# A HGRN2 head scan whose read-out is computed with tokens on the partitions

## The chip, the cores and the metric

One core of one Trainium2 chip. The metric is the device time of one execution in microseconds. The kernel before was run three times; a fourth execution was profiled.

## What is computed

A two-layer backbone over 512 latent and 256 context tokens of width 1024, all float32. Layer 0 mixes tokens with a bidirectional HGRN2, layer 1 with a Mamba-2; a SwiGLU FFN ends each. The change touches layer 0's mixer alone, 8 heads with keys and values of 128 and chunks of 64 tokens. Each direction computes

```python
cum = jnp.cumsum(lf, axis=2)
ref = cum[:, :, CHUNK // 2 - 1:CHUNK // 2]
qr = qc * jnp.exp(cum - ref)
kr = kc * jnp.exp(ref - cum)
att = jnp.where(causal, jnp.einsum('bclhd,bcshd->bchls', qr, kr), 0.0)
o_intra = jnp.einsum('bchls,bcshv->bclhv', att, vc)
ds = jnp.einsum('bcshd,bcshv->bchdv', kc * jnp.exp(last - cum), vc)
# s_in: the states, scanned over chunks with decay exp(last)
o_inter = jnp.einsum('bclhd,bchdv->bclhv', qc * jnp.exp(cum), s_in)
o = (o_intra + o_inter)
```

and the read-out is `rmsnorm(o_forward + o_backward, gn_w) * silu(g)`, the norm over a head's 128 values, and then a product with `w_out`.

## The kernel before

Activations lie feature-major: 128 features on the partitions, 768 tokens (T) along the free dimension. A weight panel is 128 output features of a weight, loaded by SP (`load_panel`, line 248), split into a rounded high part by ScalarE (`split_hi`, 254) and a low part by VectorE (`split_lo`, 258), and multiplied by `product` (261 to 284): for each of eight k steps three products of high and low parts in two halves of 384 tokens, so six matmuls on line 275. Splits run two panels ahead.

A head needs five panels, j = 0 to 4: q, gate, two forget gates, v. `hg_all` (711) is a software pipeline: while the panels of head h + 1 (called `hn_` there) are multiplied, TensorE does the scan of head h in between, after the k steps that the tables `STEP_AT` and `OUT_AT` (549, 550) name as (j, k). Heads run in pairs in a loop of three turns (`Fori`, 715); the first head has no scan beside it, and the scan of the last has no panels beside it.

The scan's steps on TensorE (`hg_tensor_scan`, 474 to 525): 1 transposes v, 2 and 3 transpose the decayed keys kd of both directions (490), 4 makes the attention blocks (503: 32-column strips of the array), 5 to 7 the state increments of chunks (515, 64 rows of the array each, even and odd chunks in different halves). VectorE masks and adds the attention of both directions into `attS` (670, 674) and runs the states into `sin` (`states`, 636 to 647).

The read-out (`hg_tensor_out`, 527 to 545) gives per chunk of 64 tokens one product with `vtm` as the stationary and `attS` as the moving operand, and one per direction with a state `sin` stationary and 64 columns of `qe` moving:

```python
pe.matmul(to, m["vtm"][o:o + CH, c // 2, :], m["attS"][o:o + CH, c // 2, :], start=True, stop=False)
for d in inter:
    ins = pe.matmul(to, sin[d][:, c, :], chunks(qe[d][:, :])[:, c, :], start=False, stop=(d == inter[-1]))
```

The profile has two records per float32 matmul. The first chunk of a direction has no state, so two of the twelve chunks have one direction. Then ScalarE copies the output to `osb` (631) and squares it into `osq` (632); TensorE sums over partitions with `ones` (step 9, 520); VectorE makes the mean (`mean_dve`, 391), GpSimd the -1/2 power (`rsqrt_pool`, 396), TensorE spreads it over partitions with the identity (`spread_pe`, step 10, 386), and VectorE multiplies twice (705, 708) into `og`. Step 9 stands after (4, 4) and step 10 after (4, 7).

VectorE in panel j = 4, in this order (680 to 709): the split, lf and th (684, 688), the two scans `cum` (694, waiting for ScalarE's Ln, 626), four offsets `kr`, `kd` (699) that ScalarE's exponentials (`decays`, 601 to 607) wait for, then the read-out's mean and the two multiplications. Step 1 of the next head waits for them (`og0`).

Of the kernel before, what the change touches and what calls it, by code (L numbers as in the profile page):

```python
# [25 lines left out]
P = 128  # L26
# [14 lines left out]
HEADS = 8  # L41
# [74 lines left out]
def memory(nc):  # L116
# [4 lines left out]
    def run(at, *items):  # L121
# [31 lines left out]
        *[(n, (P, T)) for n in ("qs", "vT", "osb", "osq")],  # L153
        *[(n, (P, NBLK, P)) for n in ("vtm", "kdtm0", "kdtm1")],
        *[(n, (P, NBLK, CH)) for n in ("att0", "att1", "attS")],
# [24 lines left out]
def program(nc, x, c, ctx_x, c_ctx, ada_w, ada_b, norm_w, ffn_w_in, ffn_w_out, final_norm_w, hg_w_in, hg_lb,  # L180
            hg_norm_w, hg_w_out, ssm_w_in, ssm_conv_w, ssm_conv_b, ssm_dt_bias, ssm_a_log, ssm_d, ssm_norm_w,
            ssm_w_out, out):
    with ExitStack() as ctx:
# [13 lines left out]
            sig lf cum dif ex kd qk vtm kdtm step cp att sf sb osq og0 og osp_hi osp_lo  # L197
# [183 lines left out]

        def spread_pe(pe, K, nb, to):
# [7 lines left out]
        def mean_dve(dve, nb, n):  # L390
            dve.tensor_scalar(m["stat"][:, 0:nb], S[:, 0, 0:nb], 1.0 / n, EPS, ALU.mult, ALU.add)\
               .then_inc(s["stat"], 1)
# [19 lines left out]
        def norm_dve(dve, xt, N, K, segs, l, i):  # L412
            sums_dve(dve, N, segs)
            dve.wait_ge(s["rbc"], K + 1)
# [42 lines left out]
        def by_parity(buf):  # L457
            return buf[:, :].rearrange("p (b q l) -> p q b l", q=2, l=CH)
# [15 lines left out]
        def hg_tensor_scan(pe, hp, h, step):  # L474
# [42 lines left out]
            elif step == 9:  # L517
                pe.wait_ge(s["osq"], h + 1)
                for b in range(NBLK):
                    ins = pe.matmul(S[:, 0, b:b + 1], block(m["osq"][:, :], b), ones[:, :],  # L520
                                    start=True, stop=True)
            else:
                spread_pe(pe, h + 1, NBLK, pair)
                return
            ins.then_inc(s["step"], 1)

        def hg_tensor_out(pe, h, n):

            c = OUT_ORDER[n]
# [17 lines left out]
        OUT_ORDER = sorted(range(NCH), key=lambda c: max(ORDER[0].index(c), ORDER[1].index(c)))  # L547
        OUT_EARLY = sum(max(ORDER[0].index(c), ORDER[1].index(c)) <= 8 for c in range(NCH))
        STEP_AT = {(0, 5): 1, (1, 0): 2, (1, 3): 3, (1, 6): 4, (2, 1): 5, (2, 3): 6, (2, 5): 7, (4, 4): 9, (4, 7): 10}
        OUT_AT = {(3 + (k - 1) // KT if k else 2, (k - 1) % KT): k for k in range(NCH)}  # L550
# [22 lines left out]
        def hg_scalar(act, hg, hn_, hp, h, pn_par, ps_par):  # L573
# [35 lines left out]
            for j in range(5):  # L609
# [40 lines left out]
        def hg_vector(dve, hg, hn_, hp, h, pn_par, ps_par):  # L650
            for j in range(5):
# [14 lines left out]
                if j == 1 and h is not None:  # L666
                    step_done(dve, h, 4)
                    dve.memset(m["carry"][:, :], 0.0)
                    for d in (0, 1):
# [4 lines left out]
                    dve.tensor_tensor(m["attS"][:, :, :], att[0][:, :, :], att[1][:, :, :], ALU.add)\  # L674
                        .then_inc(s["att"], 1)
# [14 lines left out]
                if j == 4 and hg is not None:  # L690
# [473 lines left out]
        def ss_vector(dve, ss, g, q, prev):  # L1164
            for j in range(len(PANELS)):
# [255 lines left out]
        def l1_vector(dve):  # L1421
# [22 lines left out]
            dve.wait_ge(s["rbc"], K2 + 3 + GROUPS)  # L1444
# [70 lines left out]
        def _(pool):  # L1515
# [30 lines left out]
            pool.wait_ge(s["og"], HEADS)  # L1546
# [6 lines left out]
        def _(act):  # L1553
# [13 lines left out]
            act.wait_ge(s["og"], HEADS)  # L1567
# [11 lines left out]
        def _(dve):  # L1579
# [130 lines left out]
```

## Time and profile before

| | |
|---|---|
| median of three runs | 2448.22 us (2442.34 to 2449.22) |
| the profiled execution | 2440.77 us, span 2439.0 us |
| granted TensorE clock over it | 0.945 |
| TensorE busy | 2244.6 us, 92% |
| VectorE, ScalarE busy | 1066.7 us, 843.4 us |
| line 275, three products | 718.1, 668.7 and 668.5 us |
| line 542, states | 64.7 us in 352 records |
| line 540, attention | 44.5 us in 192 records |

Times in rows are from the span's start. A record's length contains its way through the array, so records overlap and starts tell the pace; a busy TensorE is not one at its peak. "Idle before, releaser" says how long an engine had nothing to do and what ended it. The granted clock is a share of full speed: 1.00 is 2.4 GHz, 0.50 is 1.2 GHz.

### The profile page before, as it was taken

The page shows a single profiled execution, that of the slowest core. Times are in us where ns is not written, and L with a number is a line of the kernel's source. Part 1 is how long each engine was busy: PE and PEld are TensorE (multiplying, and loading weights), DVE is VectorE, ACT ScalarE, POOL GpSimd, SP SyncE. Part 2 cuts the span into 40 slices and gives each one's busy share as a digit, 9 for nine tenths or more (in the row PEclk, how much of TensorE's full clock was granted, in tenths as well). Part 3 has the DMA queues.
Part 4 walks back from the last instruction along what each step waited for, and adds up shares of the span by engine and source line. Part 5 has one row for each costly group of instructions (what it writes and reads, how often), then busy time and mean ns, then how long its engine had stood idle before and what let it go on. Part 6 is the DMA issues. An engine that isn't in the chain of part 4 may idle for free.

```text
span 2439.0 us, 34378 instructions
## 1 busy us (share of the span) xinstructions
PE 2244.6 (92%) x13554; PEld 1967.2 (81%) x13554; DVE 1066.7 (44%) x1484; ACT 843.4 (35%) x1250; POOL 39.3 (2%) x67
## 2 busy tenths in 40 slices
PE   5899999998897999999999599999997698999998
PEld 3888888887796999999999587777774476888886
DVE  5444454455334222222223756766665434333333
ACT  2443343443123332112221343737372223542222
POOL 1000000000000000000000100000000000000000
PEclk8999999999698999999999889999998598999998
DMA  6322222222222332234321121121111132332331
GB/s 261 104 79 79 70 66 66 70 64 67 78 78 93 105 112 86 61 104 129 109 74 50 52 70 44 44 61 43 52 43 43 68 102 68 98 103 87 95 111 62
DMA packets 296560, 198.03 MB, mean 81 GB/s; under 512 B 4900, under 2 KB 288925, under 8 KB 295837
## 3 DMA queue, kind: packets, MB, share of 16 engines
q1 hardware_dynamic: 293965, 180.03, 24.1%
q0 software_dynamic: 2512, 16.80, 1.8%
q8 instruction: 64, 1.05, 0.2%
q14 instruction: 19, 0.16, 0.0%
HBM read 186.32 MB, written 10.49 MB: 81 GB/s over the span
## 4 chain that ended last, share of the span: by engine, by line
PE 64%; issue 24%; DVE 7%; ACT 2%; DMA 1%; POOL 1%; SPq 0%; DVEq 0%; ACTq 0%; POOLq 0%
PE G L275 50%; PE G L308 2%; PE S L542 1%; PE S L1296 1%; PE S L386 1%; PE S L1147 1%; DVE hn L420 1%; PE S L540 1%; DVE hlo L428 1%; PE S L515 1%; PE S L1143 1%; PE S L1309 1%; POOL rstd L396 1%; ACT whi L254 1%; PE S L1298 1%
## 5 line engine op out<-in xcount | busy, mean ns | idle before, releaser
L275 PE MATMUL G<-hhi,whi 128*128 128x384 f32 (+1 forms) x2320 | 718.1, 373 | 39.2 <-DVE hlo L428 24.5
L258 DVE TENSOR_TENSOR wlo<-raw,whi 128x1024 fp32r<-128x1024 f32 (+1 forms) x225 | 288.2, 1281 | 934.4 <-ACT whi L254 934.4
L275 PE MATMUL G<-hhi,wlo 128*128 128x384 f32 (+1 forms) x2320 | 668.7, 351 | 0.0
L275 PE MATMUL G<-hlo,whi 128*128 128x384 f32 (+1 forms) x2320 | 668.5, 351 | 0.0
L254 ACT ACTIVATE whi<-raw 128x1024 fp32r<-128x1024 f32 (+1 forms) x225 | 248.9, 1107 | 1025.7 <-PE G L275 507.5
L275 PEld LDWEIGHTS G<-hhi,whi 128*128 128x128 f32 x2320 | 416.2, 192 | 99.3 <-issue 52.7
L275 PEld LDWEIGHTS G<-hhi,wlo 128*128 128x128 f32 x2320 | 429.8, 191 | 20.8
L275 PEld LDWEIGHTS G<-hlo,whi 128*128 128x128 f32 x2320 | 431.3, 191 | 18.0
L275 PE MATMUL G<-mhi,whi 128*128 128x384 f32 (+1 forms) x656 | 209.1, 362 | 13.7 <-DVE mlo L1428 13.7
L275 PE MATMUL G<-mlo,whi 128*128 128x384 f32 (+1 forms) x656 | 208.7, 361 | 0.0
L275 PE MATMUL G<-mhi,wlo 128*128 128x384 f32 (+1 forms) x656 | 208.5, 361 | 0.0
L275 PEld LDWEIGHTS G<-mhi,whi 128*128 128x128 f32 x656 | 121.2, 189 | 26.8 <-issue 11.5
L275 PEld LDWEIGHTS G<-mlo,whi 128*128 128x128 f32 x656 | 121.2, 189 | 12.0
L275 PEld LDWEIGHTS G<-mhi,wlo 128*128 128x128 f32 x656 | 121.1, 188 | 11.9
L1178 DVE SCALAR_TENSOR_TENSOR acc<-xpad,colC,acc 128x770 f32<-128x770 f32 (+1 forms) x96 | 93.7, 976 | 36.4 <-ACT acc L1064 29.1
L1036 ACT ACTIVATE e<-S,shiftT 128x128 f32<-128x128 f32 x256 | 69.5, 382 | 57.6 <-PE S L1298 57.4
L772 ACT ACTIVATE mhi<-mid 128x768 f32 (+3 forms) x44 | 32.5, 739 | 95.8 <-DVE mid L793 95.8
L542 PE MATMUL S<-qe,sin 128*128 128x64 f32 x352 | 64.7, 307 | 0.0
L647 DVE SCALAR_TENSOR_TENSOR sin<-sin,gl,S 128x128 f32<-128x128 f32 x160 | 54.9, 348 | 6.9 <-PE S L515 1.8
L542 PEld LDWEIGHTS S<-qe,sin 128*128 128x128 f32 x352 | 50.9, 206 | 7.0
L347 ACT ACTIVATE sq<-x 128x512 f32 (+3 forms) x32 | 23.5, 738 | 93.3 <-DVE x L821 66.5
L797 DVE TENSOR_TENSOR mlo<-mid,mhi 128x768 f32 (+3 forms) x44 | 36.3, 826 | 44.2 <-ACT mhi L772 44.2
(245 smaller groups left out, 2025.3 us busy)
## 6 DMA issues: line engine op xcount, KB each, us to landing
raw<-in_ffn_w_in_dram SPq DMA_DIRECT2D x88, 512.0 KB, 3.6
adaw<-in_ada_w_dram SPq DMA_DIRECT2D x40, 1024.0 KB, 5.3
raw<-in_ffn_w_out_dram SPq DMA_DIRECT2D x32, 704.0 KB, 4.2
raw<-in_ssm_w_in_dram SPq DMA_DIRECT2D x41, 512.0 KB, 3.6
raw<-in_hg_w_in_dram SPq DMA_DIRECT2D x40, 512.0 KB, 3.7
ada<-in_ada_w_dram SPq DMA_DIRECT2D x4, 2048.0 KB, 13.1
raw<-in_ssm_w_out_dram SPq DMA_DIRECT2D x16, 512.0 KB, 3.4
raw<-in_hg_w_out_dram SPq DMA_DIRECT2D x8, 512.0 KB, 3.5
```

What stands on the lines that cost most here:

```text
L254: act.activation(whi[pn.slot][:, 0:kt, :], raw[pn.slot][:, 0:kt, :], ACT.Copy).then_inc(s["hi"], 1)
L258: dve.tensor_tensor(wlo[pn.slot][:, 0:kt, :], raw[pn.slot][:, 0:kt, :], f32(whi[pn.slot][:, 0:kt, :]), ALU.subtract).then_inc(s["lo"], 1)
L275: ins = pe.matmul(G[:, tl.slot, g0:g0 + n], w[pn.slot][:, k, :], r[:, k_base + k, t0:t0 + n], start=(first and k == 0 and i == 0), stop=(l ...
L308: ins = pe.matmul(to[o:o + 2, :], m["csil"][:, k, :], w[:, k, :], start=(k < STRIPS), stop=(k >= KT - STRIPS))
L386: ins = pe.matmul(block(to, b), m["rstd"][:, b:b + 1].to_broadcast([P, P]), ident[:, :], start=True, stop=True)
L396: pool.tensor_tensor(m["rstd"][:, 0:nb], m["stat"][:, 0:nb], m["mhalf"][:, 0:nb], ALU.pow)\
L542: ins = pe.matmul(to, sin[d][:, c, :], chunks(qe[d][:, :])[:, c, :], start=False, stop=(d == inter[-1]))
L647: dve.scalar_tensor_tensor(to, sin[d][:, cc, :], gl[d][:, cc:cc + 1], new, ALU.mult, ALU.add).then_inc(own, 1)
L772: act.activation(m["mhi"][:, bass.ds(i, 1), 0:nt].rearrange("p a t -> p (a t)"), m["mid0"][:, 0:nt], ACT.Copy).then_inc(s["mhi"], 1)
L797: dve.tensor_tensor(m["mlo"][:, bass.ds(i, 1), 0:nt].rearrange("p a t -> p (a t)"), m["mid0"][:, 0:nt], f32(m["mhi"][:, bass.ds(i, 1), 0:n ...
L1036: ins = act.activation(block(m[f"e{d}{r}"][:, :], b), block(S[:, d, :], b), ACT.Exp, bias=m["shiftT"][:, b, bass.ds(q * HPG + (d * NH + hh ...
L1178: dve.scalar_tensor_tensor(m["acc"][:, 0:n], xpad[ci % 2][:, k:k + n], m["colC"][:, bass.ds(conv_tile(kind, i, g) + k * CONV_TILES, 1)], m ...
```

## The change

The read-out is written for a block of 128 tokens, two chunks, with tokens on the partitions. `attS` becomes 128 x 128 per block, with each chunk's 64 x 64 on the diagonal and zeros elsewhere (set once ahead of head 0), and is the stationary operand; `vtm` is moving. For the states, 64 columns of `qe` are stationary and the state moves with 128 columns; the even chunk uses array columns 0 to 63, the odd one 64 to 127. Mean squares are then sums along the free dimension: ScalarE squares straight from PSUM into the buffer of `vT`, VectorE reduces, and scales with `rstd` broadcast along the free dimension. Six transposes bring the result back to feature-major, and one operation applies weight and gate. Steps 9 (sums) and 10 (spread) and the `osb` copy go. `OUT_AT` puts the six blocks into panels 2 and 3.

```diff
+        *[(n, (P, T)) for n in ("qs", "vT", "osb")], ("osum", (P, 8)),
+        *[(n, (P, NBLK, CH)) for n in ("att0", "att1")], ("attS", (P, NBLK, P)),
...
+        osq = m["vT"]
...
-            elif step == 9:
-                pe.wait_ge(s["osq"], h + 1)
+            else:
+                pe.wait_ge(s["osn"], h + 1)
                 for b in range(NBLK):
-                    ins = pe.matmul(S[:, 0, b:b + 1], block(m["osq"][:, :], b), ones[:, :],
-                                    start=True, stop=True)
-            else:
-                spread_pe(pe, h + 1, NBLK, pair)
-                return
+                    ins = pe.transpose(block(pair, b), block(m["osb"][:, :], b), ident[:, :])
...
-            elif n == OUT_EARLY:
+            elif n == NBLK - LBLK:
...
-            o = CH * (c % 2)
-            to = S[:, 2 + c % 2, (c // 2) * CH:(c // 2 + 1) * CH]
-            inter = [d for d in (0, 1) if c != ORDER[d][0]]
-            pe.matmul(to, m["vtm"][o:o + CH, c // 2, :], m["attS"][o:o + CH, c // 2, :], start=True, stop=False)
-            for d in inter:
-                ins = pe.matmul(to, sin[d][:, c, :], chunks(qe[d][:, :])[:, c, :],
-                                start=False, stop=(d == inter[-1]))
-            if n == NCH - 1:
+            to = block(PAIR[1], b)
+            pe.matmul(to, m["attS"][:, b, :], m["vtm"][:, b, :], start=True, stop=False)
+            for d in (0, 1):
+                for c in (2 * b, 2 * b + 1):
+                    if c != ORDER[d][0]:
+                        o = CH * (c % 2)
+                        ins = pe.matmul(to[o:o + CH, :], chunks(qe[d][:, :])[:, c, :], sin[d][:, c, :],
+                                        start=False, stop=(d == 1 or c == ORDER[1][0]))
+            if n == NBLK - 1:
...
-        STEP_AT = {(0, 5): 1, (1, 0): 2, (1, 3): 3, (1, 6): 4, (2, 1): 5, (2, 3): 6, (2, 5): 7, (4, 4): 9, (4, 7): 10}
-        OUT_AT = {(3 + (k - 1) // KT if k else 2, (k - 1) % KT): k for k in range(NCH)}
+        OUT_ORDER = list(range(LBLK, NBLK)) + list(range(LBLK))
+        STEP_AT = {(0, 5): 1, (1, 0): 2, (1, 3): 3, (1, 6): 4, (2, 1): 5, (2, 3): 6, (2, 5): 7, (4, 7): 9}
+        OUT_AT = {(2, 7): 0, (3, 1): 1, (3, 3): 2, (3, 4): 3, (3, 5): 4, (3, 6): 5}
...
-                    act.activation(by_parity(m["osb"]), o4, ACT.Copy)
-                    act.activation(by_parity(m["osq"]), o4, ACT.Square).then_inc(s["osq"], 1)
+                    act.activation(osq[:, :], PAIR[1][:, 0:T], ACT.Square).then_inc(s["osq"], 1)
...
-                    dve.tensor_tensor(m["attS"][:, :, :], att[0][:, :, :], att[1][:, :, :], ALU.add)\
-                        .then_inc(s["att"], 1)
+                    for o in (0, CH):
+                        ins = dve.tensor_tensor(m["attS"][o:o + CH, :, o:o + CH], att[0][o:o + CH, :, :],
+                                                att[1][o:o + CH, :, :], ALU.add)
+                    ins.then_inc(s["att"], 1)
...
+                if j == 4 and h is not None:
+                    dve.wait_ge(s["osq"], h + 1)
+                    dve.tensor_reduce(m["osum"][:, 0:NBLK], by_block(osq[:, :]), axis=mybir.AxisListType.X,
+                                      op=ALU.add).then_inc(s["osr"], 1)
+                    dve.wait_ge(s["osr"], h + 1)
+                    mean_dve(dve, NBLK, P, m["osum"][:, 0:NBLK])
+                if j == 4 and hg is not None:
+                    offsets(hn_, 0)
+                if j == 4 and h is not None:
+                    dve.wait_ge(s["rstd"], h + 2)
+                    r = m["rstd"][:, 0:NBLK].rearrange("p (b a) -> p b a", a=1)
+                    dve.tensor_tensor(by_block(m["osb"][:, :]), by_block(PAIR[1][:, 0:T]),
+                                      r.to_broadcast([P, NBLK, P]), ALU.mult).then_inc(s["osn"], 1)
+                if j == 4 and hg is not None:
+                    offsets(hn_, 1)
                 if j == 4 and h is not None:
                     step_done(dve, h, 9)
-                    mean_dve(dve, NBLK, P)
-                    dve.wait_ge(s["rbc"], h + 2)
-                    dve.scalar_tensor_tensor(m["osb"][:, :], m["osb"][:, :], m["colA"][:, COL_GN:COL_GN + 1],
-                                             PAIR[1][:, 0:T], ALU.mult, ALU.mult).then_inc(s["og0"], 1)
-                    dve.wait_ge(s["og0"], h + 2)
-                    dve.tensor_tensor(m["og"][:, bass.ds(h, 1), :].rearrange("p a t -> p (a t)"),
-                                      m["osb"][:, :], gs[ps_par][:, :], ALU.mult).then_inc(s["og"], 1)
+                    dve.scalar_tensor_tensor(m["og"][:, bass.ds(h, 1), :].rearrange("p a t -> p (a t)"),
+                                             PAIR[0][:, 0:T], m["colA"][:, COL_GN:COL_GN + 1], gs[ps_par][:, :],
+                                             ALU.mult, ALU.mult).then_inc(s["og0"], 1)
...
+            dve.memset(m["attS"][:, :, :], 0.0).then_inc(s["og0"], 1)
```

`offsets(head, d)` holds the two subtractions of line 699 for one direction. The waits on `rbc` elsewhere count eight fewer spreads, and what waited for `og` now waits for `og0`.

TensorE in the fourth panel (j = 3) of a head, before; each row names the moving, then the stationary operand, and the size of the result:

```order
L275 MATMUL G<-hhi,wlo_70 128x384 x2
L540 MATMUL S<-attS,vtm 128x64
L542 MATMUL S<-qe_97,sin_119 128x64
L542 MATMUL S<-qe_98,sin_120 128x64
L275 MATMUL G<-hhi,whi_69 128x384 x2
```

and with the change:

```order
L275 MATMUL G<-hhi,wlo_70 128x384 x2
L542 MATMUL S<-vtm,attS 128x128
L547 MATMUL S<-sin_119,qe_97 64x128 x2
L547 MATMUL S<-sin_120,qe_98 64x128 x2
L275 MATMUL G<-hhi,whi_69 128x384 x2
```

One insertion now holds a block of two chunks; before, each chunk had its own, and three chunks stood in the fifth panel.

VectorE from the second scan to the product into `og`, in the panel j = 4, before:

```order
L694 SCALAR_TENSOR_TENSOR cum_106<-segm,lf_104 128x768
L699 TENSOR_TENSOR kr_93<-cum_105 128x768
L699 TENSOR_TENSOR kd_99<-cum_105 128x768
L699 TENSOR_TENSOR kr_94<-cum_106 128x768
L699 TENSOR_TENSOR kd_100<-cum_106 128x768
L571 REGISTER_ALU
L391 TENSOR_SCALAR stat<-S 128x6
L704 REGISTER_ALU
L705 SCALAR_TENSOR_TENSOR osb<-osb,colA,S 128x768
L708 ISA
L708 TENSOR_TENSOR og<-osb,gs_107 128x768
```

and with the change:

```order
L704 SCALAR_TENSOR_TENSOR cum_106<-segm,lf_104 128x768
L708 TENSOR_REDUCE osum<-vT 128x6
L395 TENSOR_SCALAR stat<-osum 128x6
L656 TENSOR_TENSOR kr_93<-cum_105 128x768
L656 TENSOR_TENSOR kd_99<-cum_105 128x768
L715 REGISTER_ALU
L717 TENSOR_TENSOR osb<-S,rstd 128x768
L656 TENSOR_TENSOR kr_94<-cum_106 128x768
L656 TENSOR_TENSOR kd_100<-cum_106 128x768
L575 REGISTER_ALU
L723 ISA
L723 SCALAR_TENSOR_TENSOR og<-S,colA,gs_107 128x768
```

The reduce and the mean now stand ahead of the offsets of direction 0, the scaling between the two directions, and the product into `og` behind the transposes that wait for the scaling. The offsets are on line 656 now, in `offsets`.

## Rows read from the trace of the kernel before

**Rows 1.** The page: busy time by engine, and the chain by engine.
```profile
PE 2244.6 (92%) x13554; PEld 1967.2 (81%) x13554; DVE 1066.7 (44%) x1484; ACT 843.4 (35%) x1250; POOL 39.3 (2%) x67
...
PE 64%; issue 24%; DVE 7%; ACT 2%; DMA 1%; POOL 1%; SPq 0%; DVEq 0%; ACTq 0%; POOLq 0%
```

**Rows 2.** Windows of single heads (us, PE, PEld, DVE, ACT, POOL busy, PEclk, DMA share, GB/s).
```profile
190.02:261.97 71.95, 68.72 (x564) 62.05 (x563) 37.29 (x57) 25.90 (x36) 1.32 (x1) 0.98 0.23 71
261.97:329.71 67.74, 66.90 (x564) 60.44 (x563) 28.87 (x49) 25.91 (x36) 1.32 (x1) 1.00 0.22 69
```

**Rows 3.** PE timeline (start, length, what, count): a step with a chunk, plain steps.
```profile
302.00 0.51 PE L275 MATMUL G<-hlo,whi 128*128 128x384 f32 x2
...
302.79 0.43 PE L540 MATMUL S<-attS,vtm 64*128 64x64 f32 x2
303.15 0.66 PE L542 MATMUL S<-qe,sin 128*128 128x64 f32 x4
...
304.06 0.51 PE L275 MATMUL G<-hlo,whi 128*128 128x384 f32 x2
...
318.22 0.51 PE L275 MATMUL G<-hlo,whi 128*128 128x384 f32 x2
...
319.26 0.51 PE L275 MATMUL G<-hlo,whi 128*128 128x384 f32 x2
```

**Rows 4.** PE timeline of the fifth panel of that head.
```profile
308.18 0.60 PE L275 MATMUL G<-hhi,whi 128*128 128x384 f32 x2
...
321.99 1.60 PE L386 MATMUL S<-ident,rstd 128*128 128x128 f32 x12 [0.84 <-POOL rstd L396]
323.35 0.59 PE L275 MATMUL G<-hhi,whi 128*128 128x384 f32 x2
```

**Rows 5.** PE timeline, other insertions of the same head.
```profile
338.51 0.82 PE L490 MATMUL S<-ident,kd 128*128 128x128 f32 x6
339.08 0.59 PE L275 MATMUL G<-hhi,whi 128*128 128x384 f32 x2
...
342.41 1.46 PE L503 MATMUL S<-qr,kr 128*32 128x64 f32 x96
...
350.98 1.16 PE L515 MATMUL S<-vtm,kdtm 64*128 64x128 f32 x16
...
354.36 0.94 PE L515 MATMUL S<-vtm,kdtm 64*128 64x128 f32 x12
```

**Rows 6.** VectorE timeline beside that fifth panel.
```profile
310.59 1.02 DVE L684 TENSOR_SCALAR lf<-th 128x768 f32<-128x768 f32 x2
...
313.60 3.41 DVE L694 TENSOR_TENSOR_SCAN cum<-segm,lf 128x768 f32<-128x768 f32 x2 [1.06 <-ACT lf L626]
316.93 0.93 DVE L699 TENSOR_TENSOR kr<-cum 128x768 f32<-128x768 f32 x1
317.78 0.95 DVE L699 TENSOR_TENSOR kd<-cum 128x768 f32<-128x768 f32 x1
...
323.64 1.01 DVE L705 SCALAR_TENSOR_TENSOR osb<-osb,colA,S 128x768 f32<-128x768 f32 x1 [3.10 <-PE S L386]
```

**Rows 7.** ScalarE timeline there.
```profile
314.56 0.81 ACT L631 ACTIVATE osb<-S 128x768 f32<-128x768 f32 x1
```

**Rows 8.** PE windows around a loop branch (us, PE busy, PEclk, DMA share, GB/s).
```profile
391.30:395.05 3.75, 0.04 (x1) 1.00 0.00 0
395.26:398.67 3.41, 3.41 (x12) 0.50 0.56 159
```

**Rows 9.** Timelines of the last head, PE and then VectorE; a window.
```profile
620.14 0.66 PE L540 MATMUL S<-attS,vtm 64*128 64x64 f32 x2 [1.28 <-issue]
...
640.85 2.72 PE L520 MATMUL S<-ones,osq 128*128 128x1 f32 x12 [1.60 <-ACT osq L632]
...
649.24 0.96 DVE L708 TENSOR_TENSOR og<-osb,gs 128x768 f32<-128x768 f32 x1
...
617.15:652.00 34.85, 26.41 (x104) 22.89 (x104) 7.58 (x20) 3.28 (x5) 1.92 (x2) 0.50 0.02 5
```

More of the change, by code:

```diff
@@ L152, in memory @@
         *[(f"{n}{d}", (P, T)) for n in ("kr", "qr", "qe", "kd", "th", "lf", "cum", "gs") for d in (0, 1)],
-        *[(n, (P, T)) for n in ("qs", "vT", "osb", "osq")],
+        *[(n, (P, T)) for n in ("qs", "vT", "osb")], ("osum", (P, 8)),
         *[(n, (P, NBLK, P)) for n in ("vtm", "kdtm0", "kdtm1")],
-        *[(n, (P, NBLK, CH)) for n in ("att0", "att1", "attS")],
+        *[(n, (P, NBLK, CH)) for n in ("att0", "att1")], ("attS", (P, NBLK, P)),
         *[(f"sin{d}", (P, NCH, P)) for d in (0, 1)], *[(f"gl{d}", (P, NCH)) for d in (0, 1)],
@@ L196, in program @@
             x sq sqd ssum stat rstd rbc hn hhi hlo
-            sig lf cum dif ex kd qk vtm kdtm step cp att sf sb osq og0 og osp_hi osp_lo
+            sig lf cum dif ex kd qk vtm kdtm step cp att sf sb osq osr osn og0 osp_hi osp_lo
             mhi mlo
@@ L380, in norm_pe, with spreads @@
             spread_pe(pe, K, nb, PAIR[1])
+        def spreads(K):
+            return K + 1 - (HEADS if K else 0)
         def spread_pe(pe, K, nb, to):
@@ L388, in spread_pe, with mean_dve @@
             ins.then_inc(s["rbc"], 1)
-        def mean_dve(dve, nb, n):
-            dve.tensor_scalar(m["stat"][:, 0:nb], S[:, 0, 0:nb], 1.0 / n, EPS, ALU.mult, ALU.add)\
+        def mean_dve(dve, nb, n, total=None):
+            dve.tensor_scalar(m["stat"][:, 0:nb], S[:, 0, 0:nb] if total is None else total, 1.0 / n, EPS, ALU.mult, ALU.add)\
                .then_inc(s["stat"], 1)
@@ L413, in norm_dve @@
             sums_dve(dve, N, segs)
-            dve.wait_ge(s["rbc"], K + 1)
+            dve.wait_ge(s["rbc"], spreads(K))
             def scaled(j):
@@ L455, in chunks, with by_block @@
             return ap.rearrange("p (c l) -> p c l", l=CH)
-        def by_parity(buf):
-            return buf[:, :].rearrange("p (b q l) -> p q b l", q=2, l=CH)
+        def by_block(ap):
+            return ap.rearrange("p (b n) -> p b n", n=P)
+        osq = m["vT"]
         def at_token(ap, t):
@@ L516, in hg_tensor_scan @@
                                     m["vtm"][o:o + CH, cc // 2, :], start=True, stop=True)
[L517 to L518 removed]
+            else:
+                pe.wait_ge(s["osn"], h + 1)
                 for b in range(NBLK):
[L520 to L524 removed]
+                    ins = pe.transpose(block(pair, b), block(m["osb"][:, :], b), ident[:, :])
             ins.then_inc(s["step"], 1)
         def hg_tensor_out(pe, h, n):
[L529 removed]
+            b = OUT_ORDER[n]
             if n == 0:
@@ L533, in hg_tensor_out @@
                 pe.wait_ge(s["att"], h + 1)
-            elif n == OUT_EARLY:
+            elif n == NBLK - LBLK:
                 for own in ("sf", "sb"):
                     pe.wait_ge(s[own], 11 * h + 11)
-            o = CH * (c % 2)
-            to = S[:, 2 + c % 2, (c // 2) * CH:(c // 2 + 1) * CH]
-            inter = [d for d in (0, 1) if c != ORDER[d][0]]
-            pe.matmul(to, m["vtm"][o:o + CH, c // 2, :], m["attS"][o:o + CH, c // 2, :], start=True, stop=False)
-            for d in inter:
-                ins = pe.matmul(to, sin[d][:, c, :], chunks(qe[d][:, :])[:, c, :],
-                                start=False, stop=(d == inter[-1]))
-            if n == NCH - 1:
+            to = block(PAIR[1], b)
[7 more added lines that the diff above has]
+            if n == NBLK - 1:
                 ins.then_inc(s["step"], 1)
-        OUT_ORDER = sorted(range(NCH), key=lambda c: max(ORDER[0].index(c), ORDER[1].index(c)))
-        OUT_EARLY = sum(max(ORDER[0].index(c), ORDER[1].index(c)) <= 8 for c in range(NCH))
-        STEP_AT = {(0, 5): 1, (1, 0): 2, (1, 3): 3, (1, 6): 4, (2, 1): 5, (2, 3): 6, (2, 5): 7, (4, 4): 9, (4, 7): 10}
-        OUT_AT = {(3 + (k - 1) // KT if k else 2, (k - 1) % KT): k for k in range(NCH)}
+        OUT_ORDER = list(range(LBLK, NBLK)) + list(range(LBLK))
+        STEP_AT = {(0, 5): 1, (1, 0): 2, (1, 3): 3, (1, 6): 4, (2, 1): 5, (2, 3): 6, (2, 5): 7, (4, 7): 9}
+        OUT_AT = {(2, 7): 0, (3, 1): 1, (3, 3): 2, (3, 4): 3, (3, 5): 4, (3, 6): 5}
         def hg_tensor(pe, hg, hn_, hp, h, pn_par, ps_par):
@@ L650, in hg_vector, with offsets @@
         def hg_vector(dve, hg, hn_, hp, h, pn_par, ps_par):
+            def offsets(head, d):
+                dve.wait_ge(s["cum"], 2 * head + d + 1)
+                for to, t in ((kr, REF[d]), (kd, LAST[d])):
+                    dve.tensor_tensor(chunks(to[d][:, :]), chunks(cum[d][:, :]),
+                                      at_token(cum[d][:, :], t), ALU.subtract).then_inc(s["dif"], 1)
             for j in range(5):
@@ L1220, in ss_vector @@
                     mean_dve(dve, LBLK, GW)
-                    dve.wait_ge(s["rbc"], q + (K2 + 2))
+                    dve.wait_ge(s["rbc"], q + spreads(K2 + 1))
                     for i_ in range(GT):
@@ L1443, in l1_vector @@
             sums_dve(dve, 4, LAT)
-            dve.wait_ge(s["rbc"], K2 + 3 + GROUPS)
+            dve.wait_ge(s["rbc"], spreads(K2 + 2 + GROUPS))
             for j in range(KT):
@@ L1545, in _ @@
                 rsqrt_pool(pool, h + 1, NBLK)
-            pool.wait_ge(s["og"], HEADS)
+            pool.wait_ge(s["og0"], HEADS + 1)
             pool.wait_ge(s["parked0"], 16)
@@ L1566, in _ @@
             hg_all(act, lambda *a: hg_scalar(act, *a))
-            act.wait_ge(s["og"], HEADS)
+            act.wait_ge(s["og0"], HEADS + 1)
             for j in range(HEADS):
@@ L1624, in _ @@
             for d in (0, 1):
-                ins = dve.memset(att[d][:, :, :], 0.0)
-            ins.then_inc(s["og0"], 1)
+                dve.memset(att[d][:, :, :], 0.0)
+            dve.memset(m["attS"][:, :, :], 0.0).then_inc(s["og0"], 1)
             dve.wait_ge(s["og0"], 1)
```

6 lines of the change are left out of this document (removed).

## The prediction

> **What bounds the kernel now.** I read the page first. TensorE is busy for 92% of the span and the chain that ended last runs mostly through it [rows 1], so work taken off TensorE counts where nothing is put in its place. Then I read the windows of single heads. From one head's value transposes to the next takes 67.74 us, and PE is busy for 66.90 of it; where the loop branches back the same stretch takes 71.95 us [rows 2]. TensorE bounds all of the head loop. The PE timeline prices what the change replaces.
>
> I measure an insertion between panel products from one hlo row to the next. A plain step of six L275 takes 319.26 - 318.22 = 1.04 us; the step that holds one chunk's read-out takes 304.06 - 302.00 = 2.06 us [rows 3]. A chunk costs 1.02 us, and one of a single direction 0.22 less, since its two L542 records are missing and the four of the row last 0.66 us at 0.11 us from start to start. Of the twelve chunks of a head, nine stand ahead of the fifth panel (j = 4) and three in it: 7 x 1.02 + 2 x 0.80 = 8.7 us and 3.06 us. The fifth panel runs from 308.18 to 323.35 [rows 4], 15.17 us: eight plain steps 8.32, three chunks 3.06, and the 3.79 left are the sums (L520) and the spread (L386), 0.84 of it idle until GpSimd's rstd.
>
> **The read-out.** A block of two chunks is now one full-array product (two records, 0.11 each, 0.22) and two pairs of 64-column products. The price of a pair that runs side by side is in the state products, which use two halves of the array's rows in the same manner: sixteen records last 1.16 us, twelve 0.94 [rows 5], so a pair (four records) costs 0.22. Four records one after another, with 128 streamed columns each, would be 0.43. That products in different columns overlap too is seen at L503: 96 records in four column strips last 1.46 us [rows 5], and one after another, with 48 columns on the mean at 0.11 for 128, they would be 3.9. Two pairs make 0.44. Changing the array's shape, in and out, I take from the chunk: of its 1.02 the six records are 0.66 at 0.11, which leaves 0.36, say 0.4. A block: 0.22 + 0.44 + 0.4 = 1.05 us; bounds 0.9 (smaller weight loads) and 1.5 (no overlap). Six blocks are 6.3 us, all ahead of the fifth panel, against 8.7: **2.4 us per head** there.
>
> **The fifth panel and its new wait.** Now nothing stands in it but eight plain steps: PE is through at 308.18 + 8.32 = 316.5 in this head's times, and stops at the six transposes for osn. Who makes osn? VectorE's scans start at 313.60 and keep it until 316.9, when the first offset starts [rows 6]; they wait for ScalarE's logarithms, which hang on the end of the fourth panel and don't move against it. The Square needs no more waiting for the read-out and fits where the osb copy was, 314.56 to 315.4 [rows 7]. Then on VectorE: the reduce of 128x768; stat 0.2 with the waits between; the two offsets of direction 0, 0.85 from start to start [rows 6], to about 319.9; the scaling from PSUM 1.0 (as L705 [rows 6]), to 321.0. GpSimd's 1.32 [rows 2] lies beside the offsets. The reduce isn't in the trace. Its bounds are 0.5, half of the two single-source passes of L684 in 1.02, and 1.7, half of the two scans [rows 6]; I take 0.95, as the passes over two tensors with the same 768 columns. The Trainium skill (VectorE: DVE Perf Modes, the perf-mode tier table) speaks against this operation: `tensor_reduce` has only its 1x mode, while a one-source fp32 pass can have 2x. By it the low end is out; at the price of a one-source pass the wait would be 0.4 shorter. No row here shows a reduce.
>
> So PE stands from 316.5 to 321.0, **4.5 us where it stood 0.84**. The transposes take what L490 takes, 0.57 to the next L275 [rows 5], so the next head begins at 321.6 and not 323.35: 1.8 us saved. Together 4.2 us per head.
>
> **The clock.** After a PE gap of 3.75 us at the loop's branch the granted clock was 0.50 for 3.41 us, in which 12 matmuls ran [rows 8], 0.28 us each against 0.17 in a plain step. Gaps of 0.84 were followed by none (clock 1.00 over a whole head [rows 2]). A gap of 4.5 us in each head will be followed by such a stretch: half of 3.41 is 1.7 us. Net 2.5 us per head. The branch back comes on top in two heads, where one slow stretch is paid already.
>
> **Who is behind the new wait.** ScalarE's decays of direction 0 start 1.1 us later (the reduce and stat stand ahead of the offsets), as its inputs do; VectorE's offsets of direction 1 end at 322.6 and og at 323.6, against 325.6 now. The next vT transposes come five steps after the wait, some 327: covered. Panel splits are two panels ahead. POOL's rstd and SP's loads have nothing new in front of them. If the five steps went, vT's transposes would wait for og. The attS sum becomes two half-height passes (about 0.5 us more) five steps or more ahead of its use; the memset of attS, no longer than a pass of 768 columns, lies ahead of head 0, under its panels. Both cost nothing there, and 0.5 once in the last head.
>
> **The last head** has no panels, so its chain is paid in full and at half clock: read-out from 620.14 to 639.2 (the sums start at 640.85 after 1.60 idle), 19.1 us; from there the square, the sums, the spread and two products until 650.2, 11.0 us; the clock is 0.50 [rows 9]. New: a block at half clock 0.43 + 0.86 + 0.4 = 1.7, six 10.2: 8.9 saved. Then Square 0.8, reduce 0.95, stat 0.3, rstd 1.4, scaling 1.0, six transposes at half clock 1.5, og 1.0: 7.0, against 11.0: 4.0 saved. VectorE enters this head about 2.0 earlier against the fourth panel, less 0.5 for attS: 1.5. Together 14.4 us.
>
> **Sum.** 2.4 (first head's read-out) + 6 x 2.5 = 15 + 14.4 = 31.8 us. The profiled execution took 2440.8 and would take 2409.0; the median of the three runs is 2448.2, 7.4 above it, and I keep that distance: **2416.5 us**.
>
> **The rivals.**
> *The clock takes a second slow stretch in each head* (0.13). The wait, the transposes and in two heads the branch stand in a row; 1.7 x 6 = 10 more: 2427. For it: in the last head gaps of 1 to 2 us keep the clock at 0.50 [rows 9]. Against: 3.75 us of gap cost one stretch only. The Trainium skill (TensorE: Matmul & The Clock Gate, PE-mode transpose) says that transposes don't count as busy for the clock in the way matmuls do; by it the wait and the transposes are one gap of 5.1 us, and 2427 would be the likelier time. A head of the kernel before, with 18 transposes among its panels, ran at 1.00 [rows 2], which neither bears it out nor speaks against it.
> *The clock holds* (0.08), as after 0.84: 10 less, 2406.
> *Column pairs run one after another* (0.10): each block 0.43 dearer, 2.6 a head over seven heads is 18, and at half clock 5 in the last: about 2440. Against it stands L503.
> *Each change of column half empties the array* (0.04), the case on the other side. Then each of four products costs as a lone one does: L540's 0.36 to the next start [rows 3] and 0.05 for its 128 columns, 0.41. A block is 0.22 + 1.65 + 0.2 = 2.05, dearer than its chunks; a head's six 12.3 against 6.3, 6.0 more in each of seven heads is 42, and some 10 more in the last: 2416.5 + 52 = 2468. It decides from 1.65 us a block, where the gain of 32 is spent. Against it: L503 changes strips with each record and shows nothing of this. The Trainium skill (TensorEngine Tiling (Array Packing), Key Properties) says that a change of mode drains the engine and a change of tile does not; by it this case doesn't occur and only my 0.4 per block does.
> Something I don't see has 0.03.
>
> **How the numbers follow.** The forecast as costed has 0.62. About 7 us (0.3%) is what a measurement of this kernel can tell from no change. The first three cases are faster; of the column case (8 us) half; so faster 0.88, same 0.07, slower 0.05. The range reaches from 2403 (clock holds, a cheap reduce and blocks of 0.95) to 2436 (second stretch, reduce of 1.7, half of the column loss); above lie most of the column case and the slower one.
>
> **What would show it.** Right: blocks near 1.05 us; at the osb transposes an idle of about 4.5 us released by the scaling; a 0.50 clock after it in each head; a period near 65 us; last read-out near 10 us. Wrong: periods over 67, two slow stretches a head, or four block products with starts 0.2 or more apart.

## The result, and the profile after

| | before | changed |
|---|---|---|
| median | 2445.56 us (four runs, 2442.34 to 2449.22) | 2408.3 us (four runs, 2403.95 to 2409.03) |
| profiled execution's span | 2439.0 us | 2405.9 us |
| from a head's value transposes to the next, without a loop branch | 67.73 to 67.79 us | 64.82 to 65.84 us |

The ratio is 0.9848, with a 95% interval of 0.9832 to 0.9863: 37 us less, where 31.8 were forecast; 2408.3 against a forecast of 2416.5 and a range of 2403 to 2436. Windows of three heads, the first with a loop branch, the other two without one (us, PE, PEld, DVE, ACT, POOL busy, PEclk, DMA share, GB/s), which answer to [rows 2], and of two stretches at the lower clock around the end of the new wait, which answer to [rows 8]:

```profile
189.71:259.11 69.40, 62.64 (x533) 57.87 (x532) 37.37 (x58) 24.96 (x35) 1.96 (x1) 0.93 0.23 69
259.11:324.95 65.84, 61.44 (x533) 57.07 (x532) 32.87 (x53) 24.96 (x35) 1.96 (x1) 0.95 0.23 73
...
180.81:184.22 3.41, 2.76 (x11) 2.76 (x12) 3.39 (x5) 3.41 (x6) 0.00 (x0) 0.50 0.00 0
313.92:320.74 6.82, 5.12 (x18) 5.12 (x19) 6.46 (x8) 6.82 (x12) 0.66 (x1) 0.50 0.00 0
458.53:523.60 65.07, 60.67 (x533) 56.30 (x532) 34.47 (x55) 24.96 (x35) 1.96 (x1) 0.97 0.24 74
```

A head has 533 PE records instead of 564, and PE is now idle for 4.4 us of it, where it was idle for 0.84. The blocks on the PE timeline, which answer to [rows 3], and the end of the fifth panel, which answers to [rows 4]:

```profile
296.07 0.38 PE L542 MATMUL S<-vtm,attS 128*128 128x128 f32 x2
296.39 0.66 PE L547 MATMUL S<-sin,qe 128*64 128x128 f32 x8
...
297.43 0.52 PE L275 MATMUL G<-hlo,whi 128*128 128x384 f32 x2
...
299.50 0.52 PE L275 MATMUL G<-hlo,whi 128*128 128x384 f32 x2
```

```profile
310.71 0.51 PE L275 MATMUL G<-hhi,wlo 128*128 128x384 f32 x2
315.62 1.54 PE L526 MATMUL S<-ident,osb 128*128 128x128 f32 x6 [4.40 <-DVE osb L717]
316.81 0.99 PE L275 MATMUL G<-hhi,whi 128*128 128x384 f32 x2
317.60 0.84 PE L275 MATMUL G<-hlo,whi 128*128 128x384 f32 x2
318.24 0.84 PE L275 MATMUL G<-hhi,wlo 128*128 128x384 f32 x2
318.88 0.84 PE L275 MATMUL G<-hhi,whi 128*128 128x384 f32 x2
```

From hlo row to hlo row a step with a block takes 2.07 us, 1.03 more than a plain one: two chunks for the price of one. The panel ends, PE waits 4.40 us for the scaling (L717, whose end the semaphore `osn` reports), and then runs at half speed: the pairs of L275 start 0.64 apart, not 0.35. The slow stretch had begun at 313.92, 1.7 us before the wait ended at 315.62. VectorE beside it, which answers to [rows 6]:

```profile
308.08 3.41 DVE L704 TENSOR_TENSOR_SCAN cum<-segm,lf 128x768 f32<-128x768 f32 x2 [1.06 <-ACT lf L630]
311.40 0.92 DVE L708 TENSOR_REDUCE osum<-vT 128x6 f32<-128x768 f32 x1
312.36 0.17 DVE L395 TENSOR_SCALAR stat<-osum 128x6 f32<-128x6 f32 x1
312.44 0.95 DVE L656 TENSOR_TENSOR kr<-cum 128x768 f32<-128x768 f32 x1
313.31 0.95 DVE L656 TENSOR_TENSOR kd<-cum 128x768 f32<-128x768 f32 x1
314.61 0.96 DVE L717 TENSOR_TENSOR osb<-S,rstd 128x768 f32<-128x768 f32 x1 [0.34 <-POOL rstd L400]
```

The links are those forecast, in the order forecast. The last head, which answers to [rows 9]:

```profile
601.27 0.77 PE L542 MATMUL S<-vtm,attS 128*128 128x128 f32 x2 [1.99 <-issue]
...
610.86 0.66 PE L547 MATMUL S<-sin,qe 128*64 128x128 f32 x8
616.02 1.54 PE L526 MATMUL S<-ident,osb 128*128 128x128 f32 x6 [4.50 <-DVE osb L717]
```

```profile
617.60 1.02 DVE L723 SCALAR_TENSOR_TENSOR og<-S,colA,gs 128x768 f32<-128x768 f32 x1 [1.64 <-PE S L526]
```

Where the time went, in the profiled executions: the seven stretches from the first head's value transposes to the last's took 478.2 us (122.23 to 600.41) and take 457.2 (124.89 to 582.13 on the same rows), 21 less. From there to the end of og it was 49.8 us and is 36.5, 13 less. The rest of the execution is 1 us longer.

### The profile page after: what moved, and what is told of

It is laid out like the page before. It is cut to its first block, busy times and chain, and to the rows that moved or that the text cites. A ratio compares the mean times of both kernels' runs of the same rounds, so it can differ in the third digit from the quotient of the medians.

```text
span 2405.9 us, 33890 instructions
## 1 busy us (share of the span) xinstructions
PE 2183.6 (91%) x13300; PEld 1921.9 (80%) x13314; DVE 1078.7 (45%) x1501; ACT 836.0 (35%) x1242; POOL 43.7 (2%) x67
## 4 chain that ended last, share of the span: by engine, by line
PE 64%; issue 23%; DVE 7%; ACT 2%; DMA 1%; POOL 1%; SPq 0%; DVEq 0%; ACTq 0%; POOLq 0%
PE G L275 51%; PE G L308 2%; PE S L1312 1%; PE S L1163 1%; PE S L547 1%; DVE hn L424 1%; DVE hlo L432 1%; PE S L521 1%; POOL rstd L400 1%; PE S L1159 1%; PE S L1325 1%; PE S L390 1%; ACT whi L254 1%; DVE cum L704 1%; PE G L314 1%
## 5 line engine op out<-in xcount | busy, mean ns | idle before, releaser
L275 PE MATMUL G<-hhi,whi 128*128 128x384 f32 (+1 forms) x2320 | 717.5, 373 | 37.7 <-DVE hlo L432 24.8
L275 PE MATMUL G<-hlo,whi 128*128 128x384 f32 (+1 forms) x2320 | 670.2, 352 | 0.0
L275 PE MATMUL G<-hhi,wlo 128*128 128x384 f32 (+1 forms) x2320 | 669.3, 352 | 0.0
L275 PEld LDWEIGHTS G<-hhi,whi 128*128 128x128 f32 x2320 | 420.6, 192 | 104.5 <-issue 57.5
L275 PEld LDWEIGHTS G<-hhi,wlo 128*128 128x128 f32 x2320 | 431.2, 191 | 20.7
L275 PEld LDWEIGHTS G<-hlo,whi 128*128 128x128 f32 x2320 | 433.3, 192 | 18.0
L275 PE MATMUL G<-mhi,whi 128*128 128x384 f32 (+1 forms) x656 | 208.7, 361 | 14.1 <-DVE mlo L1444 14.1
L275 PE MATMUL G<-mhi,wlo 128*128 128x384 f32 (+1 forms) x656 | 208.3, 361 | 0.0
L275 PE MATMUL G<-mlo,whi 128*128 128x384 f32 (+1 forms) x656 | 208.3, 361 | 0.0
L275 PEld LDWEIGHTS G<-mhi,whi 128*128 128x128 f32 x656 | 121.1, 188 | 27.3 <-issue 11.6
L275 PEld LDWEIGHTS G<-mhi,wlo 128*128 128x128 f32 x656 | 121.1, 188 | 12.1
L275 PEld LDWEIGHTS G<-mlo,whi 128*128 128x128 f32 x656 | 121.0, 188 | 11.8
L1163 PE MATMUL S<-wx,btm 128*128 128x512 f32 x80 | 44.3, 644 | 12.2 <-DVE wx L1118 12.2
L400 POOL TENSOR_TENSOR rstd<-stat,mhalf 128x6 f32<-128x6 f32 (+1 forms) x17 | 25.3, 1489 | 1648.8 <-DVE stat L395 1648.8
```

The lines of the kernel that those rows point to most:

```text
L275: ins = pe.matmul(G[:, tl.slot, g0:g0 + n], w[pn.slot][:, k, :], r[:, k_base + k, t0:t0 + n], start=(first and k == 0 and i == 0), stop=(l ...
L400: pool.tensor_tensor(m["rstd"][:, 0:nb], m["stat"][:, 0:nb], m["mhalf"][:, 0:nb], ALU.pow)\
L1163: pe.matmul(S[:, d, :], m["btm"][:, b, :], m[f"wx{d}"][:, :], start=True, stop=True).then_inc(s["ds"], 1)
```

## The experiments

Each kernel is the changed one with one edit. Times are medians; the kernel before, measured beside them, had 2442 to 2443. Times of single heads and rows are from one profiled execution of each kernel.

**The last three blocks in the fifth panel** (late).

```diff
-        OUT_AT = {(2, 7): 0, (3, 1): 1, (3, 3): 2, (3, 4): 3, (3, 5): 4, (3, 6): 5}
+        OUT_AT = {(2, 7): 0, (3, 2): 1, (3, 5): 2, (4, 1): 3, (4, 2): 4, (4, 3): 5}
```

> The last three blocks stand in the fifth panel, at (4, 1) to (4, 3), instead of the fourth. If PE's wait for osn hangs on VectorE's work alone (scans, reduce, mean, offsets) and not on the end of the read-out, the fourth panel ends 3.0 us earlier, the wait falls from 4.40 to about 1.4 us and osn comes no later against the fourth panel's end. The clock is then not lowered after it, 1.7 us or more in each head on top. Heads of 60 to 61 us against 65; in all about 30 us less than the changed kernel, 2378. If osn follows the end of the read-out, it comes 3 us later, the wait stays at 4.4 and the time at 2408.

Measured 2381.1 us, ratio 0.9735 (0.9698 to 0.9772). PE timeline, and windows of one head without and one with the loop's branch:

```profile
303.35 0.87 PE L526 MATMUL S<-ident,osb 128*128 128x128 f32 x6 [1.30 <-DVE osb L717]
```

```profile
249.92:310.31 60.39, 59.09 (x533) 54.71 (x532) 30.52 (x50) 25.09 (x35) 1.96 (x1) 1.00 0.26 79
310.31:376.59 66.28, 61.78 (x534) 57.16 (x533) 38.46 (x59) 25.09 (x35) 1.96 (x1) 0.95 0.24 73
```

The wait is 1.30 us, and in a head without a branch the clock stays at 1.00 after it. So osn does not follow the end of the read-out. The wait is 3.1 us shorter, but the head is 4.4 to 5.5 shorter than in the changed kernel: the rest goes with the clock. With a branch the head still takes 66.28, since PE then stands for 3.0 to 3.2 us at the branch, and a slow stretch of 6.8 us goes with that.

**The reduce made twice** (reduce2).

```diff
-                    dve.wait_ge(s["osr"], h + 1)
+                    dve.wait_ge(s["osr"], h * 2 + 1)
+                    dve.tensor_reduce(m["osum"][:, 0:NBLK], by_block(osq[:, :]), axis=mybir.AxisListType.X,
+                                      op=ALU.add).then_inc(s["osr"], 1)
+                    dve.wait_ge(s["osr"], h * 2 + 2)
```

> The reduce over the squares is made twice, 0.96 us more on VectorE ahead of everything that osn waits for. If PE's wait at the transposes is the end of VectorE's chain, the wait grows from 4.40 to 5.4 in each of the six heads with a successor and the time by 7 to 8 us, 2416. If ScalarE or the clock sets it, under 2 us.

Measured 2420.8 us, 12 more, with only two runs of it.

```profile
318.78 1.54 PE L526 MATMUL S<-ident,osb 128*128 128x128 f32 x6 [5.39 <-DVE osb L720]
```

The wait grew by 0.99 us, one for one: VectorE's chain sets it. The 12 us are more than the 7 to 8 expected. Part of the difference is the clock, as far as the traces tell: the slow stretches around the six waits were of 6.8 us and more, where the changed kernel had three of 3.4, two of 6.8 and one of 10.2.

**The transposes in the next head's first panel** (next). Step 0 is step 9 of the head before; `osb` is cleared once for the first head, and all counts of `step` are one higher.

```diff
-        STEP_AT = {(0, 5): 1, (1, 0): 2, ..., (4, 7): 9}
+        STEP_AT = {(0, 4): 0, (0, 7): 1, (1, 0): 2, ..., (4, 7): 9}
-                pe.wait_ge(s["osn"], h + 1)
+                pe.wait_ge(s["osn"], h + 1 + (step == 9))
-                if h is not None and (j, k) in STEP_AT:
+                if h is not None and (j, k) in STEP_AT and (hg is None or STEP_AT[j, k] != 9):
```

> The six transposes of a head stand after (0, 4) of the next head's panels, five plain steps later, and step 1 after (0, 7). Those five steps are 5.2 us, the wait was 4.40, so it goes, and with it the slow clock: 6 x (4.4 + 2) = some 38 us less than the changed kernel, near 2370, heads near 59 us. Rival: the wait only moves, to the value transposes of step 1 or the key transposes of step 2, because og is 5 us later on VectorE or VectorE's splits come too late; then under 15 us less, with a PE idle released by og or kd.

Measured 2368.1 us, ratio 0.9693 (0.9654 to 0.9733). From the repeat of this kernel further down: windows of a head with the branch and one without, and the PE timeline.

```profile
185.07:244.65 59.58, 59.16 (x533) 54.84 (x532) 34.52 (x55) 25.41 (x37) 1.96 (x1) 1.00 0.27 81
244.65:303.54 58.89, 58.89 (x534) 54.88 (x533) 34.42 (x55) 24.20 (x35) 1.96 (x1) 1.00 0.26 81
```

```profile
240.49 0.51 PE L275 MATMUL G<-hhi,wlo 128*128 128x384 f32 x2
240.84 0.82 PE L526 MATMUL S<-ident,osb 128*128 128x128 f32 x6
241.41 0.59 PE L275 MATMUL G<-hhi,whi 128*128 128x384 f32 x2
```

PE is busy for the whole of a head, 58.89 us. In the six heads that have more panels behind them the wait is gone, and came back nowhere. The head with a branch is only 0.7 to 1.1 us longer, where it was 3 to 4 in the changed kernel.

**The wait filled** (fill, fill5), **and work behind the transposes** (fillafter). Ten, five and five float32 matmuls whose result nothing uses, in the seven heads with panels. The edit of fill and fill5 is shown; in fillafter the same loop stands behind the six transposes and writes to another bank.

```diff
+                for _ in range(fill):
+                    pe.matmul(S[:, 0, :], ident[:, :], m["vtm"][:, 0:4, :].rearrange("p b n -> p (b n)"),
+                              start=True, stop=True)
                 pe.wait_ge(s["osn"], h + 1)
```

> Ten float32 matmuls of 512 columns (4.27 us at full clock), whose result nothing uses, are put ahead of PE's wait for osn in the seven heads with panels. If the wait costs its length and the slow clock after it besides, the length stays and the clock stays at 1.00: 8 to 13 us less than the changed kernel, near 2398. If the slow clock costs nothing, or comes for another reason, the time stays at 2408 and the granted clock falls as before.

Measured 2419.5 us, and not 2398. A miss, and my sum was at fault: twenty records took 8.7 us, 0.43 each, not 0.21. In this head, which has a branch, PE was busy for 67.50 of 67.50 us, at clock 1.00:

```profile
192.18:259.68 67.50, 67.50 (x554) 58.61 (x553) 34.57 (x55) 24.97 (x35) 1.96 (x1) 1.00 0.23 71
```

```profile
311.67 8.74 PE L525 MATMUL S<-vtm,ident 128*128 128x512 f32 x20
320.25 0.82 PE L529 MATMUL S<-ident,osb 128*128 128x128 f32 x6
```

So 4.3 us more work than the wait was long (8.7 - 4.4) made a head 1.7 us longer than one without a branch (65.84) and 1.9 shorter than one with it (69.40). The right number of fillers was the next run.

> Five of the ten fillers, 8.56 us for ten by the last run, so 4.28 us, just under the wait of 4.40. The run with ten had each head at 67.5 us, 58.9 without its fillers, the clock at 1.00 and no gap at the loop's branch. If a head is 58.9 of work and the wait is filled, heads are 63.3 us and the branch costs nothing: against 65.1 to 69.4 now, 1.8 to 6 us a head, 18 in all, near 2390, although PE does 4.3 us more in each head. If the slow clock cost nothing and the ten fillers only happened to end the branch's gap, heads stay at 65 and the time is near 2402.

Measured 2401.7 us (2397.4 to 2407.0), 0.9837 (0.9817 to 0.9856), against 2390 expected. Without and with the branch, and the PE timeline at the branch:

```profile
257.29:320.84 63.55, 63.43 (x543) 56.63 (x542) 30.54 (x50) 24.97 (x35) 1.96 (x1) 1.00 0.24 75
320.84:389.06 68.22, 65.25 (x543) 58.23 (x542) 38.44 (x59) 24.96 (x35) 1.96 (x1) 0.97 0.23 71
```

```profile
245.26 0.87 PE L529 MATMUL S<-ident,osb 128*128 128x128 f32 x6
249.51 1.00 PE L275 MATMUL G<-hhi,whi 128*128 128x384 f32 x2 [3.38 <-DVE wlo L258]
```

The half on the clock held: the four heads without a branch take 63.5 to 63.6 us against 64.8 to 65.8, with the same wait filled by useless work, so the slow clock costs a head 1.2 to 2.3 us. The half on the branch missed: its gap stayed.

> The same five fillers behind the six transposes. PE still waits 4.40 us and its clock falls, but at the loop's branch it now has 4.3 us of work in its queue. If the gap at the branch (2.4 and 3.1 us) comes from an empty queue it goes, or shrinks under 1 us, while heads without a branch become 4.3 us (or 6 and more at the lower clock) longer than 65. If the branch costs its time whatever is queued, both gaps stay. Time 2430 to 2440.

Measured 2430.3 us (two runs). PE timeline at the branch and windows with and without it:

```profile
250.06 1.54 PE L526 MATMUL S<-ident,osb 128*128 128x128 f32 x6 [4.40 <-DVE osb L722]
251.40 5.32 PE L529 MATMUL S<-vtm,ident 128*128 128x512 f32 x10
256.16 0.91 PE L275 MATMUL G<-hhi,whi 128*128 128x384 f32 x2
```

```profile
193.51:262.82 69.31, 64.91 (x543) 57.58 (x542) 34.58 (x54) 24.96 (x35) 1.96 (x1) 0.98 0.23 70
262.82:333.30 70.48, 66.08 (x544) 58.01 (x543) 34.57 (x54) 24.96 (x35) 1.96 (x1) 0.95 0.22 68
```

No gap is left at the branch: the head with it is no longer than the other. The six kernels agree on one condition. Where PE has just been released from a wait and has six transposes and nothing else ahead of the branch (changed, late, fill5), it stands for 2.4 to 3.4 us. Where work is queued (next, fillafter, and fill, whose fillers ran on past the release), it stands for under 1.

The traces show one thing more at the branch. The gap's row names VectorE's split `wlo`, but that split can't be what PE needs: in a head without a branch the same products start at 316.81, and the split of that place begins only at 318.25. What comes at a branch, and in the changed kernel at no other end of a head, is a transfer of 16 KB on a DMA queue of instructions. (Inside a head there are four more, and PE doesn't stop at them.) In the changed kernel it runs from 247.39 to 248.49; the DMA view of 247 to 250 us, and PE's first product behind that branch:

```profile
q8 instruction: 1, 0.02, 2.3%
...
250.13 1.00 PE L275 MATMUL G<-hhi,whi 128*128 128x384 f32 x2 [2.36 <-DVE wlo L258]
```

From 310 to 325 us, around the end of a head without a branch, that queue moves nothing. From the start of this transfer to PE's first product behind the branch it was 2.6 to 3.1 us at both branches of changed, late, fill5 and next. In next the transfer started 2.2 us before PE ran dry, in fillafter with all the fillers still to do, and in the changed kernel within 0.4 us of PE's running dry. So, as an estimate from these rows, the branch costs some 3 us less what is still queued when it is reached. That the fetched instructions are what PE waits for is read from these times; no run changed the fetch alone.

**The two halves of the array** (serial, onehalf). In serial the loops over direction and chunk change places, so that neighbours use the same half:

```diff
-            for d in (0, 1):
-                for c in (2 * b, 2 * b + 1):
+            for c in (2 * b, 2 * b + 1):
+                for d in (0, 1):
```

> Within a block both directions of the even chunk come first and then both of the odd one, so that neighbours share the array's half. If products in the two halves run side by side when they alternate, and only then, a block with four state products becomes 0.43 dearer (1.01 to 1.44) and one with three 0.22: 2.2 us per head, 15 in seven heads and 4 in the last at half clock, near 2427. If the halves do not overlap now, or overlap in either order, the time stays at 2408.

Measured 2408.1 us, the second answer: no change.

```profile
297.30 0.38 PE L542 MATMUL S<-vtm,attS 128*128 128x128 f32 x2
297.61 0.67 PE L547 MATMUL S<-sin,qe 128*64 128x128 f32 x8
```

Eight records last 0.67 us, as before. The time alone leaves open whether they overlap in any order or never. The single records say more: they start in twos, 0.01 us apart, and one pair follows another after 0.11. The next kernel settles it.

```diff
-                        ins = pe.matmul(to[o:o + CH, :], chunks(qe[d][:, :])[:, c, :], sin[d][:, c, :],
-                                        start=False, stop=(d == 1 or c == ORDER[1][0]))
+                        pe.matmul(to[0:CH, :], chunks(qe[d][:, :])[:, c, :], sin[d][:, c, :],
+                                  start=False, stop=False)
+            ins = pe.matmul(to, m["attS"][:, b, :], m["vtm"][:, b, :], start=False, stop=True)
```

> All state products of a block go into the even chunk's half (the read-out of the odd chunks is left out, and the attention product is made twice, the second time to close the block). Twice the attention product alone is 1.01 + 0.22 = 1.23 us and one more change of shape, 1.3. If the two halves run side by side in the changed kernel whatever the order, one half alone makes the four products serial: 0.43 more, 1.7 us a block, and starts 0.107 apart one by one instead of in twos. If products of 64 columns are faster than I think and nothing overlaps, the block is 1.3.

```profile
300.21 0.51 PE L275 MATMUL G<-hlo,whi 128*128 128x384 f32 x2
...
300.90 0.38 PE L542 MATMUL S<-vtm,attS 128*128 128x128 f32 x2
301.21 1.09 PE L547 MATMUL S<-sin,qe 128*64 128x128 f32 x8
302.23 0.49 PE L549 MATMUL S<-vtm,attS 128*128 128x128 f32 x2
...
302.91 0.35 PE L275 MATMUL G<-hlo,whi 128*128 128x384 f32 x1
```

The same eight records last 1.09 us in one half and 0.66 in two, 0.43 apart, and start one by one; the block takes 2.70 - 1.04 = 1.66 us. The halves run side by side, whatever the order in the program. The edit also lets all eight add into the same rows of the output; but in serial four neighbouring records do that too, at no cost. The run's 2439.4 us is 31 over the changed kernel.

**Fillers in the last head** (nexttail beside next_again). As next, with `keep_busy` ahead of six waits of the last head:

```diff
+            def keep_busy(n):
+                for _ in range(n if hg is None else 0):
+                    pe.matmul(G[:, 0, 0:EVEN], ident[:, :], m["segm"][:, 0:EVEN], start=True, stop=True)
...
+                    keep_busy({(1, 0): 2, (1, 3): 3, (1, 6): 2, (2, 5): 3, (2, 7): 3, (4, 7): 6}.get((j, k), 0))
```

> The same kernel as the run next, beside nexttail on the same chip: 2368, and against the kernel before a ratio of 0.969 to 0.970.

> As next, with fillers of 384 columns (0.64 us each at full clock) ahead of the waits of the last head, whose results nothing uses. TensorE's clock was 0.50 through nearly all of that head. If its low clock is what the six blocks (10 us there, 6 at full clock), the key transposes and the last transposes pay, keeping TensorE busy gives back 4 to 6 us, near 2363. If the chain there is VectorE's and ScalarE's and the fillers only add to it, 2368 or more.

Measured 2368.2 us for next_again (five runs, 2360.8 to 2374.1; ratio 0.9696, 0.9676 to 0.9716) and 2359.3 for nexttail (2358.2 to 2363.4; 0.966, 0.9647 to 0.9673). Windows of the last head, of the first and then the second:

```profile
531.00:575.00 44.00, 25.76 (x228) 19.56 (x226) 27.00 (x48) 11.28 (x17) 3.36 (x3) 0.61 0.04 13
```

```profile
532.00:571.00 39.00, 31.15 (x271) 20.94 (x270) 27.95 (x49) 11.91 (x18) 3.74 (x3) 0.91 0.05 14
```

The clock is 0.91 instead of 0.61, and from the last head's value transposes to the end of og it is 30.6 us instead of 36.9, 6.3 less. That is what the profiles show. The medians differ by 9, the two profiled executions (2364.5 and 2363.4) by 1 only, since everything outside the last head took 5 us longer in the second: the last head's gain is read directly, how much of it reaches the whole time is not settled. This is the fastest version, 83 us under the kernel before.

## Why the prediction was right

- **What bounds it**: TensorE, in the head loop apart from the new wait, which VectorE's chain ends (reduce2). With that wait out of the way, in next, PE is busy 58.89 of 58.89 us.
- **The block, 1.05 us**: 1.03 between hlo rows. The overlap of the halves, taken from products in halves of the rows and in strips, holds: onehalf makes it 0.43 dearer.
- **The new wait, 4.5 us**: 4.40. The reduce, taken as 0.95 between 0.5 and 1.7, lasts 0.92; the trace sides with the Trainium skill's statement (VectorE: DVE Perf Modes) that it has no faster mode, since L684 with as many columns takes 0.55. The size of one link was off: I put GpSimd's power beside the offsets at 1.32, and it took 1.96 there, which left VectorE idle for 0.34.
- **The clock**: right in kind, with the size between the forecast and the first rival. The stretches at 0.50 around the six waits were 3.4, 10.2, 6.8, 6.8, 3.4 and 3.4 us. The four heads without a branch lost 1.2, 2.3, 1.6 and 1.5 us to it (against the same heads of fill5), where 1.7 was forecast. What the forecast didn't see is that a stretch can begin inside the wait, where it costs nothing: behind the wait these four had 2.8, 5.1, 3.4 and 3.4 us of it, and half of that is 1.4, 2.6, 1.7 and 1.7. Whether the six transposes count as work for the clock no run tells apart.
- **The last head**: blocks 10.3 us (10.2 forecast) from 601.27 to 611.5, and from there to og's end at 618.6 7.1 us (7.0). From the value transposes to the first block it is 0.6 us less, where 1.5 was forecast.
- **Where I was short**: 31.8 forecast, 33.1 in the profiled executions, 37.3 between the medians. In the first, errors of the terms offset each other. The seven stretches gave 20.9 us where the sum has 17.4 (2.4 and six times 2.5), and the part behind them 13.3 where it has 14.4; the rest was 1 longer. Most of the first excess lies in the two heads with a branch, 2.6 and 4.8 us: the prediction says that they pay for one slow stretch already, and its sum charges them a new one all the same. The last stretch gave 3.4 for 2.4, which makes up for the 0.9 that the last head, behind it, gave too little. The second difference is not one of mechanism: I kept 7.4 us between the profiled execution and the median, and the changed kernel's profiled execution (2407.6) lies within 1 us of its median. So 2409.0, the sum without those 7.4, came within 1 us of the median partly by luck, since errors offset.
- **The rivals**: the column cases fell by onehalf and the block's price; the clock that holds fell with the windows at 0.50, and not by the time, since 2408.3 lies nearer to its 2406 than to 2416.5; a second slow stretch came in three of six heads, in part inside the wait or the gap at the branch.

What the prediction didn't see is that its own text held a better kernel: the wait of 4.40 us, and the clock behind it, were given away by the place of the transposes alone. Five plain steps later they cost 0.57 us, with PE busy throughout.

## What to carry to other kernels

Where the operation at the end of a chain (here six transposes) returns to the bound engine, put it as many independent steps later as the chain is longer than what hides it; the wait costs its length, the slow clock that reaches beyond it, and, in front of a loop's branch, the branch, because PE then comes to the branch with nothing queued. Small products with 64 moving columns can be turned round so that the 64 are stationary and two share the array: here two chunks for the price of one. When you fill a wait to test the clock, fill it in a measured unit (records of the same shape in the trace).

## What the runs showed of the hardware

- A float32 record streams 128 columns in 0.11 us (the starts of onehalf's eight are 0.109 apart) and 512 in 0.43 (fill); my 0.21 for 512 was wrong by two.
- Products in two halves of the columns overlap even when the program writes two for one half and then two for the other.
- The gap at the loop's branch, 2.4 to 3.7 us (3.7 in the kernel before), depends on what is queued: under 1 us, or none, with work queued behind the last wait. A transfer of 16 KB on a queue of instructions starts at the branch, and PE's first product comes 2.6 to 3.1 us after its start; at the branch of 3.7 us in the kernel before there were two such transfers, and it came after 4.3.
- Useless matmuls shortened heads twice: 4.3 us of them in place of a 4.4 us wait by 1.2 to 2.3 us a head (whole time 2401.7 against 2408.3, with intervals that overlap, so not shown for the whole), and the last head by 6.3 us (2359.3 against 2368.2).
- GpSimd's power on six columns took 1.96 us beside two VectorE passes over two tensors, and 1.32 where VectorE was waiting (the kernel before, and the last head of the changed one).
